# A two-block transformer kernel: its opening taken in four rounds of two feature blocks, with four in-projection parts open at once in PSUM

## The reference, cut to what matters

```python
mod = adaln_params(c, w_mod[layer], b_mod[layer])          # silu(c) @ w_mod + b_mod, six vectors of 1024
mod_c = adaln_params(c_ctx[None, :], w_mod[layer], b_mod[layer])
h = modulate(x, norm1_g[layer], mod[:, 0], mod[:, 1])      # rms_norm(x) * g * (1 + scale) + shift
hc = modulate(ctx, norm1_g[layer], mod_c[:, 0], mod_c[:, 1])
rq, rk, rv, rg, dq, dk, dv = jnp.split(h @ w_in[layer], IN_SPLITS, axis=-1)      # 3072 columns
crq, crk, crv, crg, cdq, cdk, cdv = jnp.split(hc @ w_in[layer], IN_SPLITS, axis=-1)
```

## Time and profile before

| | |
|---|---|
| runs of the kernel | 1319.54, 1319.56, 1320.89 us; median 1319.56 us |
| profiled execution, own time | 1320.18 us |
| its span in the trace | 1318.4 us |
| busy share TensorE, VectorE, ScalarE, GpSimd | 87%, 59%, 30%, 22% |
| mean rate of the transfers | 339 GB/s |

### The profile page before, as it was taken

One profiled execution on the slowest core, in us unless ns is written; L12 is line 12 of the kernel. 1 busy time (PEld: TensorE's weight loads), 2 busy tenths in 40 slices (PEclk: granted clock), 3 DMA queues, 4 the chain that ended last, 5 costly groups with the idle time before them and its releaser, 6 DMA issues.

```text
span 1318.4 us, 16268 instructions
## 1 busy us (share of the span) xinstructions
PE 1142.0 (87%) x5864; PEld 702.0 (53%) x5864; DVE 771.4 (59%) x1976; ACT 392.9 (30%) x1100; POOL 295.5 (22%) x278
## 2 busy tenths in 40 slices
PE   6999999999988998877777777779999999867896
PEld 4887889855554554432222233227888885323342
DVE  2798786889767766777767677444842516211121
ACT  2213441346323333233333233223521513000011
POOL 0100000344434344444443444330030000000000
PEclk9999999999999999999999999999999999988999
DMA  9844366799999999999999999998421477999996
GB/s 391 332 158 160 113 241 253 283 421 421 421 420 423 421 421 418 421 412 419 421 405 423 417 412 403 421 381 350 133 97 33 192 303 281 426 424 424 425 385 251
DMA packets 60283, 446.78 MB, mean 339 GB/s; under 512 B 6704, under 2 KB 7088, under 8 KB 10160
## 3 DMA queue, kind: packets, MB, share of 16 engines
q0 software_dynamic: 36864, 268.45, 49.3%
q1 hardware_dynamic: 22912, 175.97, 33.1%
q10 hardware_dynamic: 432, 1.40, 0.3%
HBM read 444.74 MB, written 1.05 MB: 338 GB/s over the span
## 4 chain that ended last, share of the span: by engine, by line
PE 44%; DMA 37%; DVE 11%; ACT 4%; issue 2%; POOL 0%; SPq 0%; DVEq 0%; ACTq 0%
DMA wring<-uv_in,arena 18%; PE bank L2768 11%; DMA arena<-uv_in,arena 9%; PE bank L2610 6%; DMA wring<-moe_in 5%; PE bank L2867 4%; DVE arena L2055 4%; PE bank L3117 3%; PE bank L3133 2%; PE bank L3075 2%; DMA arena<-moe_in 2%; DMA arena<-ctxT_in 2%; PE bank L2864 2%; PE bank L3103 1%; PE bank L3139 1%
## 5 line engine op out<-in xcount | busy, mean ns | idle before, releaser
L2768 PE MATMUL bank<-wring,arena 128*128 128x512 f32 x512 | 244.5, 613 | 54.0 <-ACT arena L1188 54.0
L2768 PE MATMUL bank<-arena 128*128 128x512 f32 x512 | 239.0, 612 | 50.5 <-ACT arena L1188 50.5
L892 POOL DMA_INDIRECT arena<-uv_in,arena x128 | 146.4, 1144 | 353.9 <-DVE arena L1929 195.5
L2055 DVE CUSTOM_DVE_ANT_0 arena<-wring,arena 128x1024 f32<-128x1024 f32 x128 | 156.9, 1226 | 89.1 <-DMA wring<-uv_in,arena 89.1
L2055 DVE CUSTOM_DVE_ANT_0 arena<-arena 128x1024 f32<-128x1024 f32 x128 | 156.9, 1226 | 88.2 <-DMA arena<-uv_in,arena 87.5
L2768 PEld LDWEIGHTS bank<-arena 128*128 128x128 f32 x512 | 94.7, 193 | 182.7 <-issue 96.2
L2768 PEld LDWEIGHTS bank<-wring,arena 128*128 128x128 f32 x512 | 92.1, 194 | 167.2 <-ACT arena L1188 85.0
L892 POOL DMA_INDIRECT wring<-uv_in,arena x128 | 130.4, 1018 | 206.2 <-PE bank L2768 197.4
L1180 ACT ACTIVATE arena<-arena 128x2 f32<-128x2 f32 x127 | 26.0, 205 | 400.3 <-DVE arena L2055 400.2
L2610 PE MATMUL bank<-wring,arena 128*128 128x256 f32 x576 | 126.5, 380 | 2.4 <-DMA wring<-stream_in 1.4
L2610 PEld LDWEIGHTS bank<-wring,arena 128*128 128x128 f32 x576 | 108.9, 190 | 17.9 <-DMA wring<-stream_in 1.9
(11 more groups left out here) (509 smaller groups left out, 1530.1 us busy)
## 6 DMA issues: line engine op xcount, KB each, us to landing
wring<-stream_in SPq DMA_DIRECT2D x61, 1024.0 KB, 8.2
wring<-moe_in SPq DMA_DIRECT2D x14, 2048.0 KB, 17.7
arena<-moe_in SPq DMA_DIRECT2D x26, 1024.0 KB, 18.3
arena<-moe_in SPq DMA_DIRECT2D x12, 2048.0 KB, 18.9
wring<-moe_in SPq DMA_DIRECT2D x13, 1024.0 KB, 14.1
arena<-stream_in SPq DMA_DIRECT2D x6, 1024.0 KB, 7.2
arena<-uv_in,arena POOLq DMA_INDIRECT x128, 12.8
wring<-uv_in,arena POOLq DMA_INDIRECT x128, 12.8
```

What stands on the lines that cost most here:

```text
L892: pool.indirect_dma_start(G[j], None, uv_d, src).then_inc(gathered[j], 16)
L2055: v.tensor_tensor_reduce(out=junk, in0=G[j][:, 0:D], in1=h2[:, t, :], scale=1.0, scalar=0.0, op0=ALU.mult, op1=ALU.add, accum_out=dots[:, ...
L2768: ins = mm(bank[1 + 2 * tile + c][:, :], diag[:, j, :], G[j][:, D + c * 512:D + (c + 1) * 512], start=begins and j == 0, stop=False, skip_ ...
```

## The change

The eight modulation chunks and the first four in-projection chunks are no longer taken one after the other. There are four rounds (`ROUNDS`), each for two feature blocks (`PER_ROUND`). A round brings one shift chunk, one scale chunk, and the rows of its two feature blocks of four in-projection chunks in one transfer of 1 MB (128 x 4 x 512, so 2 KB at a time). In each round `mod_products(r)` makes shift and scale for two blocks, `round_turn(r)` turns them, VectorE modulates two blocks, and `open_part(r, c)` adds these two blocks to part c, for c = 0 to 3. The four parts stand open in banks 1 to 4 until the last round. The context is loaded ahead of the last round, its squares and the tokens' are halved by VectorE (`squares_sum`) and no longer by GpSimd, and its root, reciprocal and multiplication stand ahead of the last round's modulation. The parts 4 and 5 are now the context parts of chunks 8 and 9.

```diff
     if n < C_IN1:
-        return n
+        return OPEN + n % (WSLOTS - OPEN)
-IN1_PARTS = [(place, n, ctx) for place, n in enumerate(IN1_ORDER)
-             for ctx in ((False, True) if n in CTX_CHUNKS else (False,))]
+IN1_PARTS = [(place, n, False) for place, n in enumerate(IN1_ORDER[:OPEN])]
+IN1_PARTS += [(place, n, True) for place, n in enumerate(IN1_ORDER[:OPEN]) if n in CTX_CHUNKS]
+IN1_PARTS += [(place, n, ctx) for place, n in enumerate(IN1_ORDER) if place >= OPEN
+              for ctx in ((False, True) if n in CTX_CHUNKS else (False,))]
+def part_bank(q):
+
+    return 1 + q if q < OPEN else 1 + q % 2
...
+        def mod_products(pe, r):
+
+            for g in range(2):
+                n = 2 * r + g
...
+        def round_turn(pe, r):
+
+            pe.wait_ge(mod_out, r + 1)
+            pe.wait_ge(cond_pick, 2)
+            for i in range(2 * PER_ROUND):
...
```

SyncE's opening:

```diff
+            for r in range(ROUNDS):
+                if r == ROUNDS - 1:
+                    sp.wait_ge(x_here, 32)
+                    sp.dma_start(chT, ctxT_d).then_inc(x_here, 16)
+                for g in range(2):
+                    n = 2 * r + g
+                    s = chunk_slot(n)
+                    if n >= WSLOTS - OPEN:
+                        sp.wait_ge(chunk_used, n - (WSLOTS - OPEN) + 1)
+                    sp.dma_start(wring[:, s * CHUNK:(s + 1) * CHUNK], wstream_d[g * MOD_GROUP + r])\
+                      .then_inc(chunk_here[s], 16)
+                ks = slice(r * PER_ROUND * COLS, (r + 1) * PER_ROUND * COLS)
+                sp.dma_start(opening[:, :, ks], wstream_d[first:first + OPEN, :, ks].rearrange("n p c -> p n c"))\
+                  .then_inc(chunk_here[r], 16)
```

ScalarE's:

```diff
+            def modulation_out(r):
+
+                chunk_done(act, 2 * r + 1)
+                if r >= 2:
+                    act.wait_ge(mod_turned, r - 1)
...
+            for r in range(ROUNDS):
+                if r == ROUNDS - 1:
+                    act.dma_start(rows[:, :], rows_d).then_inc(const_here, 16)
+                    act.wait_ge(x_here, 48)
+                    nc.scalar.activation(csq, chT, ACT.Square).then_inc(inputs_ready, 1)
+                    input_root(1)
+                modulation_out(r)
```

VectorE's:

```diff
+            for r in range(ROUNDS):
+                if r == ROUNDS - 1:
+                    dve.wait_ge(inputs_ready, 3)
+                    squares_sum(csq)
+                    dve.wait_ge(rms_root, 2)
+                    link(v.reciprocal(rstd[:, 1], rstd[:, 1]))
+                    link(times_root(1, chT, chT, slice(0, KD)))
+                modulation_round(r)
+                shifted(0, hT, range(PER_ROUND * r, PER_ROUND * (r + 1)))
+                if r == 0:
+                    link(times_root(0, xT, hT, slice(PER_ROUND, KD)))
+            shifted(1, chT)
```

TensorE's:

```diff
+            def open_part(r, c):
+
+                if c == 0:
+                    pe.wait_ge(chunk_here[r], 16)
+                w = slot_view(c)
+                for t in range(NT):
+                    for k in range(PER_ROUND * r, PER_ROUND * (r + 1)):
+                        if c == 0 and t == 0:
+                            pe.wait_ge(h_ready, k + 1)
+                        ins = mm(bank[part_bank(c)][:, t * COLS:(t + 1) * COLS], hT[:, k, t * P:(t + 1) * P], w[:, k, :],
+                                 start=k == 0 and t == 0, stop=k == KD - 1, skip_group_check=True)
+                if r == ROUNDS - 1:
+                    ins.then_inc(proj_done if IN1_ORDER[c] in CTX_CHUNKS else chunk_used, 1)
...
+            mod_products(pe, 0)
+            input_sum(0, sq)
+            round_turn(pe, 0)
+            unread(6, 2, 256)
+            for r in range(ROUNDS):
+                open_part(r, 0)
+                if r == ROUNDS - 2:
+                    input_sum(1, csq)
+                if r < ROUNDS - 1:
+                    mod_products(pe, r + 1)
+                open_part(r, 1)
+                open_part(r, 2)
+                if r < ROUNDS - 1:
+                    round_turn(pe, r + 1)
+                open_part(r, 3)
```

More of the change, by code:

```diff
@@ L50 @@
 C_IN2 = C_Q + N_Q + N_SK
[L52 removed]
+ROUNDS = MOD_GROUP
+PER_ROUND = KD // ROUNDS
+OPEN = 4
 C_OUT2 = C_IN2 + N_IN2
@@ L681, in two_blocks @@
         MOD_BANK = (0, 7, 3, 3, 6, 0)
-        def mod_products(pe, g, banks, chunks=range(MOD_GROUP)):
-            for n in chunks:
-                chunk_ready(pe, C_MOD[g] + n)
-                w = wchunk(C_MOD[g] + n)
+        def mod_products(pe, r):
+            for g in range(2):
+                n = 2 * r + g
+                chunk_ready(pe, n)
+                w = wchunk(n)
                 for k in range(KD):
                     q = k % 4
-                    ins = nc.tensor.matmul(
-                        bank[banks[n // 2]][32 * q:32 * q + 32, (n % 2) * COLS:(n % 2 + 1) * COLS],
-                        condS[:, k, :], w[:, k, :], start=k < 4, stop=k >= KD - 4)
+                    ins = nc.tensor.matmul(bank[5 + r % 2][32 * q:32 * q + 32, g * COLS:(g + 1) * COLS],
+                                           condS[:, k, :], w[:, k, :], start=k < 4, stop=k >= KD - 4)
@@ L710, in mod_turn @@
+        def mod_turn(pe, g):
+            pe.wait_ge(mod_summed, (g - 1) * MOD_GROUP)
+            for k in range(KD):
+                ins = nc.tensor.matmul(bank[MOD_BANK[g]][:, 2 * k:2 * k + 2],
+                                       mod_sums[g - 2][k // 2][:, (k % 2) * P:(k % 2 + 1) * P], ones[:, 0:2],
+                                       start=True, stop=True)
             ins.then_inc(mod_turned, 1)
@@ L722, in _ @@
             sp.dma_start(xT, xT_d).then_inc(x_here, 16)
-            for n in range(WSLOTS):
-                sp.dma_start(wring[:, n * CHUNK:(n + 1) * CHUNK], wstream_d[n]).then_inc(chunk_here[n], 16)
-            sp.wait_ge(x_here, 32)
+            opening = wring[:, 0:OPEN * CHUNK].rearrange("p (n c) -> p n c", n=OPEN)
+            first = C_IN1 + IN1_ORDER[0]
+            for r in range(ROUNDS):
[12 more added lines that the diff above has]
+                  .then_inc(chunk_here[r], 16)
+            sp.dma_start(const[:, CN_FIRST:], const_d[:, CN_FIRST:]).then_inc(const_here, 16)
             def summed_in(m):
```

137 lines of the change are left out of this document (43 added, 94 removed).

## The result

| | median | runs | against before |
|---|---|---|---|
| before | 1319.6 us | 6, 1319.07 to 1320.89 | |
| after | 1327.13 us | 6, 1324.71 to 1328.04 | 1.0049, 95% interval 1.0039 to 1.006 |

The change makes the kernel 7.5 us slower, where I forecast 2.2 us slower; 1327.13 lies outside my range (1317.5 to 1325.8). The profiled execution took 1328.04 us of its own time.

The account below looks back on a forecast made before the run. TensorE and VectorE were taken to bound the kernel up to `roped` together, at about 102.8 us. Later `mod_sum` +0.3, opening clock +0.7 and clock at `roped` +1.2 gave +2.2 us, 1321.8 us, range 1317.5 to 1325.8.

Parts of the forecast that it names:

- The frame: Up to `roped`: TensorE and VectorE arrive together at about 102.8 us, so speeding up one alone gains nothing.
- rival 2: Up to `roped`: TensorE's gain passes on, all of 5.5 us arrives, 1314.1 us; chance 0.11.
- The opening's order: TensorE's opening: first quarter starts at 18.1 us, a round takes 9.8 us.
- The decay work's two small products: VectorE, opening: 0.2 us each in place of 2.37 and 1.31, as GpSimd has no halvings after the change.
- TensorE's clock, in the opening: First quarter and the products behind it may run at the slow pace: up to 3.6 us, taken as +0.7.
- All behind it is VectorE's own chain and as long as before: VectorE from the first `mod_sum` on: no added time, so the delay ahead of it is handed on to `roped`.
- At `roped`: Turning of the heads: TensorE idles 6.5 us, its clock falls and the turning runs slowly, +1.2 us.
- My sum: Whole kernel: +0.3 +0.7 +1.2 = +2.2 us, with delays at the opening's end handed on unchanged.
- Rival 1: Opening and `roped`: the clock holds and the opening runs at full pace, +0.3, 1319.9 us; chance 0.23.
- Rival 3: Opening: 2 KB pieces at half the rate make transfers bound the rounds, 3.5 us on VectorE's path, 1325.3 us; chance 0.20.
- Rival 4: Opening not shorter: slow clock throughout, or stalls from banks and order, 6 us or more, 1328 us; chance 0.05.

Follow-up runs that it names:

- the two edits on both kernels: One `mod_sum` moved from ahead of `roped` to later, or one more in-projection part ahead of the heads: changed kernel 1323.79, 1323.56 us; kernel before 1324.5, 1326.36.
- the first filler: Changed kernel with two filler matmuls ahead of TensorE's first turn and four, in place of two, behind it: 1322.36 us, ratio 1.0021.
- the earlier turn and both fillers: Changed kernel with filler matmuls in the opening and before the wait for `roped`, each round's turn one quarter part earlier: 1323.61 us, ratio 1.0026.
- heads from part 11: One more in-projection part ahead of the heads on TensorE: kernel before 1326.36 us (1.0044), changed kernel 1323.56 us (1.0032).
- pieces of 2 KB: Kernel before with its first four in-projection chunks loaded in four transfers of 2 KB pieces: 1338.81 us in one run.
- the kernel with both: Changed kernel with filler matmuls in the opening and sixteen more before TensorE's wait for `roped`: 1324.33 us, ratio 1.0038.

## Why the prediction was wrong

**The frame was right.** That both engines arrive at `roped` together, and that a gain of TensorE alone is worth nothing, is shown by the two edits on both kernels. TensorE won 3.6 us and none of it came through (rival 2 fell). The whole miss is 7.8 - 2.2 = 5.6 us of span: 2.0 in the first failed step, 1.4 in the second, 1.3 and 0.8 in what no term covered, 0.1 at `roped`.

**The opening's order: right.** I forecast the first quarter at 18.1 (17.82), rounds of 9.8 us (9.86, from 24.15 to 34.01). The decay work's two small products took 0.17 and 0.22 us as against 2.37 and 1.31. By the Trainium skill ("SBUF — State Buffer", section "Who interferes with whom") they were held by GpSimd's halvings; with those gone the trace agrees.

**Failed step 1: the term "TensorE's clock, in the opening", +0.7 us.** The mechanism was named, its size was taken near the wrong end of my bounds of 0 to 3.6. It measured 2.7: 1.85 in the quarter (3.75 against 1.9) and 0.8 in the products (2.72 against 1.93). My reason for the low value, "TensorE has work for most of the time", was no measure of anything: it was busy for 2.38 of 3.40 us and the clock fell. The filler brought the quarter to 1.89 us and 3.9 us off the median. The last turn came to VectorE at 49.24, where 46.5 and 0.7 were reckoned; the 2 us more are this. It is a cost of its own size in each run: the five traces with this opening that were not shifted as a whole have the last turn at 47.07 to 50.45.

**Failed step 2: "All behind it is VectorE's own chain and as long as before".** It is not its own chain: `mod_sum(2)` and `mod_sum(4)` wait for transfers that start when a slot comes free and then take longer than the one `mod_sum` that hides them. I had seen these waits (18.39 of 21.30 us busy) and held them constant. They were 1.5 us longer, 3.13 in place of 1.66 (the whole stretch 1.4 longer). In the other kernels with rounds they were between 1.86 and 3.93 us, so this is a cost that varies from one to the next; it is the time that a transfer takes to land (4.7 us before, 5.73 after), and what sets that stays open.

**At `roped`: right.** I forecast 6.5 us idle and +1.2; it was 7.95 us and +1.3, and filler removed it. The granted clock was 0.65 in the idle time and 0.60 in the turning. The Trainium skill's rule on waits between bursts ("TensorE: Matmul & The Clock Gate", section "HAM oscillation — how this bites in real kernels") fits here. In the opening the gaps were of 1.05 and 0.66 us only, and it is the trace that shows the low clock behind them.

**What no term covered.** The slow stretch at 214 us (+1.3) appears in both traces of the change (3.34 and 3.76 us for the 16 records), with the first filler (3.66) and with the earlier turn and both fillers (3.39). It does not appear in the traces of eight other kernels with rounds or in before (2.03 each), and it does in two of the three variants of the kernel before (3.50 with heads from part 11, 3.66 with pieces of 2 KB). So it isn't bound to the rounds. That thin stretches downstream meet the clock at another moment when the chain moves by some microseconds would fit, but no run tests it. My sum assumed that a delay is handed on unchanged.

**Rivals.** Rival 1 (clock holds, +0.3): refuted for the change as made; with filler, `mod_sum` at 57.35 in the kernel with both is near its forecast of 56.9 to 57.3 (58.18 with the first alone), but the medians are not near 1319.9. Rival 3 (transfers bound the rounds) gave nearly the measured time by a wrong cause: TensorE never waited for them in the rounds, and 383 to 419 GB/s were moved. Rival 4 (opening not shorter, 1328) has the nearest time. It named a slow clock throughout; in fact it was slow for 6.4 us from the first quarter on, and the tenth part was still 3.6 us earlier.

## What to carry to other kernels

When a reordering thins out TensorE's work, price the clock at the full slow pace for what comes behind, unless a row shows a stretch as thin that kept it; a few filler matmuls where the gap is are cheap, if they end before the data arrive. Before calling a chain "as long as before", list what in it waits for a transfer whose cover is one instruction. And when two engines meet at one point, test with an edit on each side, on both kernels: the one that helps one kernel and hurts the other names the late engine.

## What was unexpected of the hardware

- A transfer of 144 KB at the end of a full queue landed 12.1 to 12.4 us after its issue in the three kernels with sixteen filler matmuls far ahead of it, and 10.6 to 10.8 us in the others; the cause is open.
- A 1 MB transfer alone on the queue took 4.7 us (before), 5.7 (after) and up to 6.9 (after, with heads from part 11) from issue to landing.
- The same eight filler records took 1.97 us in one kernel and 3.64 in another with the same opening; the unfilled quarter took 2.51 to 3.75 us in six traces of one opening.
